# Four-layer diffusion trunk on one core: two QKV layers in another order, and modulation products moved from TensorE to GpSimd

## The reference

```python
m = silu(cvec) @ w_mod[i] + b_mod[i]           # 1024 -> 6144, for 2 vectors
sh1, sc1, g1, sh2, sc2, g2 = split(m, 6)
h = rmsnorm(x, norm1_g[i]) * (1 + sc1) + sh1
qkv = h @ w_qkv                                # layers 1, 3: 1024 + 256 + 256 columns
q, k, v = rmsnorm(q, qn), rmsnorm(k, kn), v    # per head of 64
q, k = rope(q), rope(k)                        # latent tokens only
x = x + g1 * (attend(q, k_all, v_all) @ w_o)   # k_all: cache of 128 and the new keys
h = rmsnorm(x, norm2_g[i]) * (1 + sc2) + sh2
u = conv3(h @ ffn_w_in) + conv_b;  a, b = split(u)
x = x + g2 * ((silu(a) * b) @ ffn_w_out)
```

## Time and profile before

| | before |
|---|---|
| median of 3 runs (from, to) | 3136.57 us (3134.68, 3139.5) |
| profiled execution: its time | 3136.35 us |
| its span | 3134.6 us |
| PE, PEld busy | 97%, 89% (21670 matmuls) |
| DVE busy | 66% |
| ACT busy | 35% |
| POOL busy | 13% (404.3 us, 392 instructions) |
| chain that ended last | PE 89%, DVE 5%, ACT 2%, DMA 2%, issue 1% |
| granted clock of TensorE | 1.0 nearly everywhere |
| DMA | 290.20 MB, mean 93 GB/s |

### The profile page before, as it was taken

One profiled execution on the slowest core, in us unless ns is written; L12 is line 12 of the kernel. 1 busy time (PEld: TensorE's weight loads), 2 busy tenths in 40 slices (PEclk: granted clock), 3 DMA queues, 4 the chain that ended last, 5 costly groups with the idle time before them and its releaser, 6 DMA issues.

```text
span 3134.6 us, 55312 instructions
## 1 busy us (share of the span) xinstructions
PE 3050.2 (97%) x21670; PEld 2793.6 (89%) x21670; DVE 2077.8 (66%) x4004; ACT 1081.9 (35%) x2250; POOL 404.3 (13%) x392
## 2 busy tenths in 40 slices
PE   8999999999999999999999899999999989999999
PEld 6899999886699999998876699999998769999999
DVE  7766666777757666668657566656667775766665
ACT  3322223336633222324335432222223663422221
POOL 3000000133310000003237310000012231000000
PEclk9999999999999999999999999999999999999999
DMA  8533323110023332331200223233231002122211
GB/s 340 217 121 120 120 103 125 61 58 1 19 104 135 121 124 103 121 108 48 79 32 8 86 104 111 107 132 120 95 116 54 4 1 95 68 81 80 67 67 48
DMA packets 47202, 290.20 MB, mean 93 GB/s; under 512 B 4945, under 2 KB 11345, under 8 KB 13265
## 3 DMA queue, kind: packets, MB, share of 16 engines
q1 hardware_dynamic: 47058, 288.21, 25.4%
HBM read 283.98 MB, written 4.21 MB: 92 GB/s over the span
## 4 chain that ended last, share of the span: by engine, by line
PE 89%; DVE 5%; ACT 2%; DMA 2%; issue 1%; POOL 0%; SPq 0%; POOLq 0%; DVEq 0%; ACTq 0%
PE psA L2014 38%; PE psB L2014 24%; PE psA L2123 4%; PE psA L2124 3%; PE psA L2129 3%; PE psB L2031 2%; PE psB L741 2%; PE psA L811 2%; PE psA L2200 1%; DMA w_stage<-weights_dram 1%; PE psB L723 1%; PE psB L869 1%; PE psA L709 1%; PE psA L2205 1%; DVE top L1623 1%
## 5 line engine op out<-in xcount | busy, mean ns | idle before, releaser
L2014 PE MATMUL psA<-h_hi,w_hi 128*128 128x320 f32 (+1 forms) x2736 | 624.9, 310 | 2.5 <-ACT u_raw L2367 1.7
L2014 PE MATMUL psA<-h_lo,w_hi 128*128 128x320 f32 (+1 forms) x2720 | 620.4, 309 | 0.0
L2014 PE MATMUL psA<-h_hi,w_lo 128*128 128x320 f32 x2704 | 616.0, 309 | 0.0
L2554 DVE SCALAR_TENSOR_TENSOR xT<-psB,mod,xT 128x128 f32<-128x128 f32 x750 | 377.7, 546 | 221.6 <-PE psB L2014 221.6
L2014 PEld LDWEIGHTS psA<-h_hi,w_hi 128*128 128x128 f32 x2736 | 456.1, 188 | 4.2 <-ACT u_raw L2367 2.5
L2014 PEld LDWEIGHTS psA<-h_lo,w_hi 128*128 128x128 f32 x2720 | 455.1, 188 | 0.0
L2014 PEld LDWEIGHTS psA<-h_hi,w_lo 128*128 128x128 f32 x2704 | 452.1, 188 | 0.0
L2613 DVE TENSOR_SCALAR conv<-u_raw,vec_sb 128x642 f32<-128x642 f32 x176 | 108.3, 615 | 438.8 <-ACT u_raw L2367 438.8
L2431 DVE TENSOR_TENSOR w_lo<-w_stage,w_hi 128x512 fp32r<-128x512 f32 x496 | 353.0, 756 | 38.1 <-ACT w_hi L2282 38.0
L2014 PE MATMUL psB<-g_hi,wo_hi 128*128 128x320 f32 x1280 | 299.3, 315 | 0.1
L2014 PE MATMUL psB<-g_hi,wo_lo 128*128 128x320 f32 x1280 | 295.3, 312 | 0.0
(11 more groups left out here) (272 smaller groups left out, 4976.2 us busy)
## 6 DMA issues: line engine op xcount, KB each, us to landing
w_stage<-weights_dram SPq DMA_DIRECT2D x124, 1024.0 KB, 5.1
m_stage<-w_mod_dram SPq DMA_DIRECT2D x96, 1024.0 KB, 8.3
wo_stage<-w_out_dram SPq DMA_DIRECT2D x44, 1024.0 KB, 4.7
yT_dram<-xT SPq DMA_DIRECT2D x8, 322.0 KB, 2.2
xT<-xT_dram SPq DMA_DIRECT2D x1, 1544.0 KB, 9.8
xT<-xT_dram SPq DMA_DIRECT2D x1, 1032.0 KB, 6.3
w_stage<-weights_dram SPq DMA_DIRECT2D x2, 512.0 KB, 17.6
rope_raw<-rope_dram SPq DMA_DIRECT2D x3, 256.0 KB, 2.6
```

Source lines behind the costliest of these rows:

```text
L2014: ins = pe.matmul(o, wp, xp[:, a:b], start=first and n == 0, stop=last and n == 2)
L2554: ins = dve.scalar_tensor_tensor(out=xT[:, d, c:c + w], in0=tokens(ps, slot)[i], scalar=gate[:, d, i:i + 1], in1=xT[:, d, c:c + w], op0=AL ...
```

## The change

**QKV of layers 1 and 3.** The chunks come in the order keys and values, queries 0, queries 1 (`QKV_ORDER`, and `SOURCE` for what SP loads). s_qkv rises three times instead of once: keys ready, first query chunk ready, all ready. The attention's entry (key_prep, query_prep and their takes on ACT and DVE) stands inside the last chunk, before its tiles 2 and 4. Of the last tile, DVE does the means in slot 3 of the attention and the rotation in slots 6 to 9; GpSimd's factor for it stands before unit 3. keep_on is gone at the entry. ACT runs one Exp of one column at the start of QKV in layers 1 to 3.

**Modulation passes.** In passes 1 to 9 of layers 0 to 2, GpSimd multiplies channels 0 to 5 of m_stage with the two conditioning values and adds them into mod_acc (two buffers of 512 columns, which lie where the norm's buffers do). PE multiplies channels 6 and 7 and picks the two sums with a one-column matrix. PE waits for s_macc before both halves. Passes 0, 10 and 11 are as before.

```diff
+POOL_PASSES = 9
+POOL_KT = 6
+QKV_ORDER = {1: (2, 0, 1), 2: range(6), 3: (2, 0, 1)}
+KV_READY = {1: 1, 2: 4, 3: 5}
+Q_READY = {1: 2, 3: 6}
+QKV_READY = {1: 3, 2: 4, 3: 7}
...
@@ TensorE, attention_pe
-            keep_on(pe, 20, OUT_LAT)
-            pe.wait_ge(s_qkv, l)
-            key_prep(0, 0)
-            key_prep(0, 1)
-            query_prep(0)
-            keep_on(pe, 11, OUT_LAT)
-            for s in SLOTS:
...
+            def entry_keys():
+                pe.wait_ge(s_qkv, KV_READY[l])
+                key_prep(0, 0)
+                key_prep(0, 1)
+            def entry_query():
+                pe.wait_ge(s_qkv, Q_READY[l])
+                query_prep(0)
...
@@ TensorE, QKV
+                            if l != 2 and (c, j) == (2, 2):
+                                entry_keys()
+                            if l != 2 and (c, j) == (2, NT - 1):
+                                entry_query()
...
@@ VectorE, qkv_dve and attention_dve
+                    if l != 2 and j == 1:
+                        ready((KV_READY if c == 1 else Q_READY)[l])
+                    if l != 2 and (c, j) == (2, 2):
+                        entry_keys()
+                    if l != 2 and (c, j) == (2, NT - 1):
+                        entry_query()
+                        rotate(i - 1)
+                        return (lambda: means(i), lambda part: rotate(i, (part,)), lambda: ready(QKV_READY[l]))
...
+                    if s == 3:
+                        last_means()
+                    if 6 <= s < 9:
+                        last_rotate(s - 6)
+                    if s == 9:
+                        last_ready()
...
@@ ScalarE, QKV
+                    own(act.activation(table_in[:, :], ones2[:, 0:1], ACT.Exp))
...
@@ GpSimd
+            def mod_added(l, i):
+                for g in range(2):
+                    pool.wait_ge(s_m[0][g], i * 16 + 16 * (6 + MOD_PASSES * l + 1))
+                for k in range(POOL_KT):
+                    dst = mod_prod[k % 2] if k else mod_acc
+                    for c in range(2):
+                        w = m_stage[0][:, :, k, :]
+                        if k == 0 and c == 0:
+                            pool_own(pool.tensor_tensor(dst[c][:, :, :], w, cond[:, k, c:c + 1].unsqueeze(2)
+                                                        .to_broadcast([P, 2, 2 * P]), ALU.mult))
+                        else:
+                            pool_own(pool.tensor_scalar(dst[c][:, :, :], w, cond[:, k, c:c + 1], 1.0, ALU.mult, ALU.mult))
+                    for c in range(2 if k else 0):
+                        last = k == POOL_KT - 1 and c == 1
+                        pool.wait_ge(s_pown, pool_own.loop + (pool_own.n - (not last)))
+                        ins = pool.tensor_tensor(mod_acc[c][:, :, :], mod_acc[c][:, :, :], dst[c][:, :, :], ALU.add)
+                        if not last:
+                            pool_own(ins)
+                ins.then_inc(s_macc, 1)
...
+                    pool.wait_ge(s_h, KT * (2 * l + 1))
+                    mod_added(l, 1)
...
+                    with pool.Fori(2, POOL_PASSES + 1) as i:
+                        pool_own.loop = (i - 2) * per
+                        pool.wait_ge(s_mraw, i * 2 + 2 * MOD_PASSES * (l + 1))
+                        mod_added(l, i)
...
@@ TensorE, out_pass
+            def mod_added(l, it, g):
+                pe.wait_ge(s_macc, it + POOL_PASSES * l)
+                for b, out in enumerate(beside(g)):
+                    n = slice(b * P, (b + 1) * P)
+                    for k in range(POOL_KT, KT):
+                        i = k - POOL_KT
+                        q = slice(32 * (i % 2), 32 * (i % 2 + 1))
+                        pe.matmul(out[q, :], cond[:, k, :], m_stage[0][:, g, k, n], start=(i < 2), stop=(k >= KT - 2))
+                    for c in range(2):
+                        q = slice(32 * (2 + c), 32 * (3 + c))
+                        ins = pe.matmul(out[q, :], pick[:, c, :], mod_acc[c][:, g, n], start=True, stop=True)
+                ins.then_inc(s_mraw, 1)
...
-                                mod_ffn(l, it + 1, d % 2)
+                                mod_added(l, it + 1, d % 2)
```

More of the change, by code:

```diff
@@ L1517, in means, with rotate @@
                                   ALU.add).then_inc(s_qms[l], 1)
-            def rotate(i):
-                c, j, n = NORMED[l][i]
+            def rotate(i, parts=range(3)):
+                _, c, j, n = NORMED[l][i]
                 is_key = c >= 2
@@ L1531, in rotate @@
                 ra, rb = rope_a[:, 0:n * DH], rope_b[:, 0:n * DH]
[L1532 to L1535, removed]
+                if 1 in parts:
+                    own(dve.tensor_tensor(ra.rearrange("p (h n) -> p h n", n=DH), xh,
+                                          rope_cos[:, int(is_key), j - 1, :].unsqueeze(1).to_broadcast([P, n, DH]),
+                                          ALU.mult))
+                for hf in range(2 if 1 in parts else 0):
                     def part(b, f):
@@ L1540, in rotate, with ready @@
                                           sn.unsqueeze(1).to_broadcast([P, n, 2, 16]), ALU.mult))
+                if 2 in parts:
+                    own.wait()
+                    own(dve.tensor_tensor(x, ra, rb, ALU.add))
+            def ready(count):
                 own.wait()
-                own(dve.tensor_tensor(x, ra, rb, ALU.add))
-            index = {(c, j): i for i, (c, j, _) in enumerate(NORMED[l])}
+                dve.tensor_copy(mark[:, count:count + 1], ones2[:, 0:1]).then_inc(s_qkv, 1)
+            index = {(p, j): i for i, (p, _, j, _) in enumerate(NORMED[l])}
             done = 3
@@ L1572, in qkv_dve @@
             rotate(done)
-            own.wait()
             dve.wait_ge(s_qe[l], nq * NT)
-            dve.tensor_copy(mark[:, l:l + 1], ones2[:, 0:1]).then_inc(s_qkv, 1)
+            ready(QKV_READY[l])
         def lo_part(dve, out, src, hi):
@@ L1582, in attention_dve @@
             kv = qkv[3]
-            if l == 3:
-                own(dve.tensor_scalar(nsink[:, :], row[:, R_SINK:R_SINK + HEADS], -1.0, None, ALU.mult))
-                own.wait()
             def take(dst, src, hi, *key):
@@ L1709, in attention_diff_dve @@
+            return entry_keys, lambda: query_pair(0), run
         def attention_diff_dve(dve, own, l, lo_first):
@@ L1975, in _, with qk_pow @@
                     pool_gpsimd(pool, pool_own)
-                for i in range(len(NORMED[l])):
-                    n = NORMED[l][i][2]
+                def qk_pow(i):
+                    n = NORMED[l][i][3]
                     pool.wait_ge(s_qms[l], i + 1)
@@ L2562, in _ @@
             own(dve.memset(ones2[:, :], 1.0))
+            own(dve.memset(pick[:, :, :], 0.0))
+            own.wait()
+            for c in range(2):
+                own(dve.memset(pick[:, c, c:c + 1], 1.0))
             own(dve.memset(hits[:, :, :], 0.0))
```

215 lines of the change are left out of this document (133 added, 82 removed).

## The result

The changed kernel takes 3268.94 us (median of 4 runs, 3267.99 to 3273.23), the kernel before 3135.88 us on the same occasion: a ratio of 1.042, 95% interval 1.041 to 1.044. Forecast were 3217 us, 3103 to 3325. The profiled execution took 3273.23 us with a span of 3271.3 us, 136.7 us more than before.

What follows compares the result with a forecast made beforehand. The prediction took PE as the bound (97% busy, 89% of the chain). From 3136.4 us it took 27 for PE's matmuls, added 116 of stall and took 8 for the entry: 3217 us, 2.6% slower, range 3103 to 3325.

Steps and rivals of the forecast that it cites:

- PE's saving: Modulation passes: 16 instead of 32 matmuls a half save PE 1.0 us a pass, 27 us in all.
- DVE's queue: Conv start to add_out: 14 DVE instructions each wait 0.78 us beside GpSimd, 10.9 against 4.9 slack, 6.0 us late.
- GpSimd's queue: Modulation sums: 28.4 us of exclusive work at the measured 81% in 25.8 us, late by 2.6 us a pass.
- the middle of 6.0 and 2.6: Modulation passes: the stall taken between the latenesses of DVE and GpSimd, 4.3 us a pass; bounds 0 and 9.3.
- the stall in sum: All 27 changed modulation passes of layers 0 to 2: 4.3 us each, 116 us added.
- the one behind 205.21: Pass with weights issued at 205.21, landed at 214.2, next pass wanted at 240.0: 25.8 us for GpSimd's 21.2.
- one row in which GpSimd adds: sq_sum on POOL, 1.71 us, beside a w_lo of 2.08 us: DVE stood still 1.39 us, 81% of POOL's instruction.
- rival 1: Modulation passes: POOL's waits fall into DVE's gaps, PE never sees them; 3101 us, faster, chance 0.23.
- an addition of 1.1 us: GpSimd's 512-column addition by the skill's rule: 1.5 us off POOL's pass, yet said to speak for a longer stall.
- 6.1 forecast: Attention entry, layers 1 and 3: 12.1 us removed, 3.0 of transposes put back, DVE's maximum 3.0 after the last product.
- the 1.9 charged for the rest: Attention slots 3 to 9: half of the 3.8 us of last-tile work moved onto busy DVE, 1.9 us a layer.
- The gain of 8: QKV with keys first, layers 1 and 3: 4.2 us gained a layer, 8 us for both.

Runs made afterwards that it cites:

- the entry alone: Only the new QKV order with the attention's entry in its last chunk, modulation passes left as before, against the kernel before: 3140.24 us, 1.0009.
- the work behind the ramp: Against the changed QKV without the modulation change: GpSimd's last factor before unit 12, rotation in slots 14, 17, 20; 3131.7 us with filler products, 3129.85 without.

## Why the prediction was right, and where it was not

- **Direction and mechanism** held: DVE stands still beside GpSimd, its adds come late, PE waits for xT before out tile 2. The numbers to look for came close: GpSimd's pass 28.6 us (26 to 31), the iteration 49.1 (48.5), PE's saving 0.84 to 0.88 us a pass (1.0).
- **DVE's queue.** I had 10.9 us of standing up to the add for out tile 2, against 4.9 of slack, so 6.0 late. In the iteration above the same 14 instructions grew by 7.1 us, and PE waited 2.45 there, so the slack was about right and the stretch a third too long. The rest of the 4.4 us are waits before out tiles 3 and 5, which I had not counted.
- **GpSimd's queue.** 2.6 us late in every pass was wrong: as DVE holds PE up, the sums come in time. PE waited for them in the first pass of each layer, in the third of layers 0 and 1 (3.2 and 3.1 us), and in most passes of the kernel whose DVE adds are moved ahead (1.1 to 1.2 us, and 3.9 to 4.0 in one pass of each layer).
- **Luck.** My 4.3 us a pass was the middle of 6.0 and 2.6. Neither was measured, and that the middle lies beside the measured 4.4 is luck.
- **The term that was mis-sized** is the stall in sum: 27 x 4.3 = 116 us forecast, 134.1 + 27 x 0.86 = 157 measured, 5.8 a pass. 4.4 is the steady part. I had reckoned every pass as the one behind 205.21. But the first weights of a layer land only 18.5 and 17.1 us before their use in layers 0 and 1 of the kernel before, where a steady pass has 25.8, and the 21.2 us of GpSimd don't fit into that even alone; PE waited 7.0 to 9.4 us. I also missed that waits of this length bring the clock down.
- **Which instructions.** I counted all 22 alike, from one row in which GpSimd adds. The ten additions do most of it; the twelve products alone hold DVE up for 2.2 us a pass, and PE not at all. In number the two errors nearly cancel, since the additions are the longer ones, but beside the products rival 1 (DVE goes first) was nearer the truth. The Trainium skill (SBUF — State Buffer, section Who interferes with whom) has a VectorE instruction with two SBUF inputs contend with a GpSimd one that reads SBUF: the trace agrees for additions (1.749 us), and beside products it shows w_lo nearly untouched in the changed kernel (0.720) and longer by 0.4 us in half of the cases in the kernel with products alone. Its sentence on tensor_scalar in a 2-port mode would fit the conv start's 0.899 against 0.615; that the conv start runs in that mode no run shows.
- **A wrong sign.** The prediction gives an addition of 1.1 us as a reason for a longer stall; it is a shorter addition than my 1.25, so it speaks for a shorter one. The shortest in the trace takes 1.26.
- **The entry.** The 5.8 us up to the first maximum were right (6.1 forecast, 12.1 - 3.0 - 3.0); the 1.9 charged for the rest were not. From the first maximum to the last, the entry alone lost 6.6 us in layer 1 and 10.1 in layer 3. GpSimd's queue is 1.0 and 2.4 of that (3.4 a layer by the medians), and even with the work behind the ramp 4.0 to 4.6 us go. The gain of 8 became a loss of 3.6 us by the medians (3140.24 against 3136.65). I had named GpSimd's factor in no step, though its wait stands in the order, ahead of unit 3.

## What to carry to other kernels

Before handing work to an idle GpSimd, list VectorE's two-input SBUF instructions in the same stretch and its slack until TensorE needs it: ten additions of 512 columns with four products took 9.3 us out of VectorE here and TensorE lost as much as with all 22 instructions, while twelve products took 2.2 us, which fitted into the slack. For the first pass of a loop, compute the time from its load to its use by itself. And work that was moved out of a critical entry into a busy pipeline cost about its length there, and 1 to 3 us a layer more where GpSimd, in order, had to wait for it.

## What the hardware showed unexpectedly

- Beside GpSimd's tensor_scalar of 512 columns, VectorE's two-input instructions keep their time or take 0.2 to 0.4 us longer, and GpSimd's stretches; beside its tensor_tensor addition VectorE's take 0.7 to 1.1 us longer. Why the form decides isn't shown. Two inputs and a long time alone don't do it: a w_lo that lies inside GpSimd's power of 128x8 values (a tensor_tensor of 1.64 to 2.01 us, kernel before) keeps its 0.68 to 0.69 us.
- GpSimd's power of 128x8 values takes 1.65 us, longer than its addition of 512 columns alone (1.26, the shortest in the trace).
- In the changed kernel TensorE's granted clock fell to 0.50 at each of its eight waits of 3.1 us or more, and at most, but not all, of those of 2.3 to 2.8 us. Iterations of 49.1 us occur at a mean clock of 1.00, with three waits, and of 0.97, with one: the slower stretch stands where the later waits would.
